# Weight blocks stored column by column in turn, and weight loads that take every other column

## The chip, the cores and the metric

The kernel runs on one core of one Trainium2 chip. The metric is the device time of one execution in microseconds (us). The kernel before took 3267.18 us, the median of three runs from 3265.66 to 3271.96 us. A core has a TensorE (PE, the matrix engine), a VectorE (DVE), a ScalarE (ACT), a GpSimd (POOL) and a SyncE (SP), which here only issues transfers. SBUF is the on-chip memory of 128 partitions that all of them read.

## The reference

The reference is a chain of transformer layers over one sequence of 256 tokens with a model width of 1024 in float32. There are two layers with half feed-forward blocks around a sparse attention and an RWKV mixer, a hybrid layer (state space and attention, then attention to a memory, with layer norms), and two layers over 272 tokens (16 meta tokens added) with a gated linear attention and a sliding-window attention. Most of the arithmetic is in feed-forward blocks of this kind, ten of them:

```python
def macaron_half_ffn(x, pre_g, post_g, w_gate, w_up, w_down):
    h = rmsnorm(x, pre_g)
    h = (jax.nn.silu(h @ w_gate) * (h @ w_up)) @ w_down
    return x + 0.5 * rmsnorm(h, post_g)
```

with `w_gate` and `w_up` of 1024 x 2816 and `w_down` of 2816 x 1024.

## The kernel before

**Tiling.** Activations lie transposed, features on the partitions and tokens along the free axis: `X[:, k, 0:T]` is block k of 128 features for T = 256 (or 272) tokens. A product is computed as output block (128 features x T tokens) = sum over k of (weight block 128 x 128) times (activation block 128 x T). The weight block is what TensorE loads (LDWEIGHTS, PEld in the profile), and the activation block is what it streams (MATMUL, PE).

**Three matmuls for one.** Weights and activations are split into a high part, rounded to the matrix engine's fast float32 format, and a low part, the rest. `mm3` (L187) issues high weight x high activation, high weight x low activation and low weight x high activation. Each issues its own weight load, and so the two in a row with the same high weight load it twice.

**Units.** Weights come from DRAM in units of 128 partitions x 1024 floats (512 KB), laid out by the host before the launch. `colunits` (L4296) makes a unit that holds the eight 128 x 128 blocks of one output block. `rowunits` (L4301) makes a unit of 128 rows of the weight with its 1024 columns, the eight blocks of eight output blocks. In both, block k is the 128 neighbouring floats k*128 to k*128+127 of each partition.

**The ring.** Class `Weights` (L200) holds eight raw slots and five slots for high parts; the low part overwrites the raw unit. SP issues the transfers in order (`load`, L240) and waits for `done`, which the last matmul of a unit raises. ACT rounds the raw unit (`hi`, L247), DVE subtracts for two of three units and POOL for the third (`low`, L256), each over the whole 1024 contiguous floats. A few units near the end of a product have their high part in spare slots instead.

**Who takes blocks.** `col` (L237) gives block k of a unit, high and low. It is used by `Ffn.firsts` (L981), `Ffn.unit` (L995), `Mixer.lin` (L1146), `Mixer.first` (L1157) and others. `Down.pe` (L927) slices its blocks itself. Some products use the weights as the streamed operand instead, 512 columns at a time: the RWKV projections (L1734), the values of the memory attention (L3153) and a few more. These read `views` of a unit and stream it.

**Addresses.** Buffers begin at chosen places within a row of 256 bytes: streamed activations at byte 64 (`PHASE`, L22), weights at byte 128 (`WPHASE`). A slot of 1024 floats is 4096 bytes, a block 512 bytes, and an activation block of 256 floats 1024 bytes, so that every block keeps its buffer's place in that row. With 272 tokens the blocks of most buffers are 320 floats apart, 1280 bytes, which keeps the place too.

**Order.** There is no planner. Each stage's methods `pe`, `act`, `dve`, `pool` give every engine its program in order, and semaphores tie them. In a feed-forward block TensorE computes gate and up blocks, 24 matmuls for a unit, then the down product.

Of the kernel before, what the change touches and what calls it, by code (L numbers as in the profile page):

```python
# [8 lines left out]
P = 128  # L9
# [190 lines left out]
class Weights:  # L200
# [34 lines left out]
        return self.his[w], self.lo_[:, r:r + UNIT]  # L235

    def col(self, w, k):  # L237
        return [x[:, k * P:(k + 1) * P] for x in self.views(w)]

    def load(self, sp, start, end=None):  # L240
        for w in range(start, len(self.units) if end is None else end):
# [32 lines left out]
    def need(self, pe, w):  # L274
        if w % 3 == 2:
            pe.wait_ge(self.cvp, w // 3 + 1)
        else:
            pe.wait_ge(self.cvl, w - w // 3 + 1)
# [5 lines left out]
class K:  # L284
# [31 lines left out]
    def hold(self, pe, bank, n):  # L316

        for _ in range(n):
            pe.mm(self.ps[bank][:, 0:P], self.ident, self.ident)
# [132 lines left out]
class Store:  # L452
# [5 lines left out]
    def pe(self, pe):  # L458
        pass
# [447 lines left out]
class Down:  # L907
# [22 lines left out]
    def pe(self, pe):  # L930
        K, T, nk = self.K, self.T, self.nk
        ends = nk > 8
        groups = [range(3)] * ends + [(k,) for k in range(3 * ends, nk - 3)] + [range(nk - 3, nk)]
        for ks in groups:
            for n in range(8):
                if self.free and ks[0] == 0:
                    pe.wait_ge(*self.free(n))
                for k in ks:
                    K.W.need(pe, self.u + k)
                    pe.wait_ge(*self.ready(k))  # L940
                    w = [x[:, n * P:(n + 1) * P] for x in K.W.views(self.u + k)]
                    t = pe.mm3(self.ps(n)[:, 0:T], w, [x[:, k, 0:T] for x in self.src], k == 0, k == nk - 1)
                    if n == 7:
                        t.then_inc(K.W.done, 1)
                    elif k == nk - 1:
                        t.then_inc(self.fin.h, 1)
# [2419 lines left out]
class Gla(Mixer):  # L3366
# [225 lines left out]
    def part(self, act, h):  # L3592
        act.wait_ge(*self.og(h))
        act.act(self.mix[0][:, 2 * h:2 * h + 2, 0:T3], self.os[:, h % 3], ACT.Copy).then_inc(self.oh.h, 1)
# [698 lines left out]
            store.pe(pe)  # L4293


def colunits(w):  # L4296
    k, n = w.shape
    return w.reshape(k // P, P, n // P, P).transpose(2, 1, 0, 3).reshape(n // P, P, k)


def rowunits(w):  # L4301
    k, n = w.shape
    return w.reshape(k // P, P, n)


def tiled(a):

    return a.reshape(len(a), D // P, P).transpose(2, 1, 0).reshape(P, -1)


def layout(v):
    d = {"x": tiled(v["x"][0]), "cst": constants(), "meta_tokens_3": tiled(v["meta_tokens_3"])}
    cols = np.zeros((P, NCOL + P), np.float32)
    cols[:, NCOL:] = np.concatenate([v["l0_cmp_w2_k"], v["l0_cmp_w2_v"]], 1)
    for name, (at, n) in COLS.items():
        a = np.repeat(v["d_skip_2"].reshape(-1), 64) if name == "d_skip_2c" else v[name]
        cols[:, at:at + n] = np.asarray(a).reshape(n, P).T
    d["cols"] = cols
    d["rows"] = np.concatenate([np.asarray(v[n]).reshape(1, 16) for n in ROWS], 1)
    for f in FFNS:  # L4320
        d[f + "_w_gate"] = colunits(v[f + "_w_gate"])
        d[f + "_w_up"] = colunits(v[f + "_w_up"])
        d[f + "_w_down"] = rowunits(v[f + "_w_down"])
    for f in ("ffn1", "ffn2"):
        w = v[f + "_w_in_2"][0]
        d[f + "_w_gate_2"] = colunits(w[:, :FF])
        d[f + "_w_up_2"] = colunits(w[:, FF:])
        d[f + "_w_out_2"] = rowunits(v[f + "_w_out_2"][0])
    for a in range(2):
        for b in range(2):  # L4330
            w = v["w_ffn_in_3"][a, b]
            d[f"g3_{a}{b}"] = colunits(w[:, :FF])
            d[f"u3_{a}{b}"] = colunits(w[:, FF:])
            d[f"d3_{a}{b}"] = rowunits(v["w_ffn_out_3"][a, b])
    w = v["l0_w_in"]
    c = np.cumsum([0, 512, 24, 128, 128, 128, 128, 128, 128, 512, 512, 512])
    part = lambda i: w[:, c[i]:c[i + 1]]
    d["nsa_in"] = colunits(np.concatenate([part(i) for i in (0, 2, 3, 4, 6, 8, 9, 10)], 1))
    d["nsa_v"] = np.concatenate([part(5), part(7)], 1).reshape(2, 4, P, 256).transpose(0, 2, 1, 3).reshape(2, P, UNIT)
    d["nsa_g"] = part(1).reshape(8, P, 24).transpose(1, 0, 2).reshape(P, 192)  # L4340
    for s in "kv":
        d["cmp_w1_" + s] = v["l0_cmp_w1_" + s].reshape(16, P, P).transpose(1, 0, 2).reshape(P, SLOT)
    d["nsa_out"] = rowunits(v["l0_w_out"])
    d["lora1"] = np.concatenate([v["l1_w_dec1"], v["l1_w_a1"], v["l1_w_g1"]], 1).reshape(8, P, 256).transpose(
        1, 0, 2).reshape(P, SLOT)
    d["lora2"] = np.concatenate([np.concatenate([v["l1_w_dec2"], v["l1_w_a2"]], 1),
                                 np.concatenate([v["l1_w0"], v["l1_a0"]])[None]], 0)
    d["l1_w_g2"] = v["l1_w_g2"]
    for n in ("l1_w_r", "l1_w_k", "l1_w_v", "l1_w_o"):
        d[n] = rowunits(v[n])  # L4350
    for n in ("l1_k_k", "l1_k_a", "l1_r_k", "l1_lnx_g", "l1_lnx_b"):
        d[n] = v[n].reshape(1, D)
    w = v["w_in_2"][0]
    c = np.cumsum([0, 1024, 1024, 1024, 2048, 16, 1024, 256, 1024, 64, 16])
    part = lambda i: w[:, c[i]:c[i + 1]]
    for i, n in ((0, "g_ssd"), (1, "g_att"), (2, "z_2"), (3, "xbc"), (5, "q_2"), (6, "ckv"), (7, "qidx")):
        d[n] = colunits(part(i))
    d["tokw"] = np.concatenate([part(4), part(9)], 1).reshape(8, P, 32).transpose(1, 0, 2).reshape(P, 256)
    d["kidx"] = part(8).reshape(8, P, 64).transpose(1, 0, 2).reshape(P, 512)
    d["w_uk"] = v["w_uk_2"][0].transpose(2, 0, 1).reshape(2, P, D)  # L4360
    d["w_uv"] = v["w_uv_2"][0].transpose(1, 0, 2).reshape(2, P, D)
    for n in ("w_proj_ssd_2", "w_proj_att_2", "w_out_2"):
        d[n] = rowunits(v[n][0])
    d["mem_2"] = tiled(v["mem_2"][0])
    d["mq"] = colunits(v["w_mq_2"][0])
    d["mk"] = colunits(v["w_mkv_2"][0][:, :D])
    d["mv"] = rowunits(v["w_mkv_2"][0][:, D:])
    d["w_mo"] = rowunits(v["w_mo_2"][0])
    w = v["gla_w_in_3"][0]
    d["gla_qk"] = colunits(w[:, :1024])  # L4370
    d["gla_v"] = colunits(w[:, 1024:2048])
    d["gla_r"] = colunits(w[:, 2048:3072])
    d["gla_lr"] = w[:, 3072:].reshape(8, P, 16).transpose(1, 0, 2).reshape(P, 128)
    d["gla_gate"] = v["gla_w_gate_3"][0]
    d["gla_out"] = rowunits(v["gla_w_out_3"][0])
    d["w_kv"] = colunits(v["w_kv_3"])
    d["swa_q"] = colunits(v["swa_w_q_3"][0])
    d["swa_out"] = rowunits(v["swa_w_out_3"][0])
    return {n: np.ascontiguousarray(a) for n, a in d.items()}


# [9 lines left out]
```

## Time and profile before

| | |
|---|---|
| Median of the runs | 3267.18 us |
| Span of the profiled execution | 3253.4 us |
| PE busy | 3111.1 us (96%), 27478 matmuls |
| PEld busy | 2988.1 us (92%), 27478 weight loads |
| DVE, ACT, POOL busy | 55%, 47%, 28% |
| DMA | 484.55 MB, mean 149 GB/s |
| Mean granted TensorE clock | 0.977 of full speed |

The profile gives no time of its own for the profiled execution beyond its span; the median lies 13.8 us above the span. The table gives shares of the span. Matmuls overlap each other in the records, and a PE that is busy for 96% says only that some matmul is nearly always in flight. The pace is to be read from the distance between the starts of matmuls, in the timeline, or from the number of matmuls that a view of windows counts in a stretch. A window counts each matmul that overlaps it, so the distance is the window's length plus one matmul's duration, divided by the count.

### The profile page before, as it was taken

The numbers are of one execution on the slowest core, as the hardware profiler recorded it, in microseconds if no ns is written. First come the engines' busy times: TensorE is split into PE (matmuls) and PEld (weight loads), VectorE is DVE, ScalarE is ACT, GpSimd is POOL, SyncE is SP. The second block draws the span as 40 slices with busy tenths as digits, with TensorE's granted clock in tenths as the row PEclk, the third lists the DMA queues.
The fourth block names the chain that finished last, engine by engine and source line by source line (L and its number), as shares of the span: only waits on it lengthen the run. The fifth ranks groups of instructions, "written<-read, shape, count | busy, mean of one in ns | idle before, by whom it ended". The sixth has DMA issues, their size and how long they took to land.

```text
span 3253.4 us, 64299 instructions
## 1 busy us (share of the span) xinstructions
PE 3111.1 (96%) x27478; PEld 2988.1 (92%) x27478; DVE 1803.0 (55%) x3040; ACT 1523.1 (47%) x2564; POOL 907.7 (28%) x481
## 2 busy tenths in 40 slices
PE   8999999999899999998999999999989999998999
PEld 8998899998688999998898889999979999997898
DVE  5456555647765645447567544454543546556554
ACT  5444454543422544437656444444333544544453
POOL 3321132331333232322221213222213332332232
PEclk9999999999999999999999999999989999998999
DMA  6542355564201555553343435535423454552354
GB/s 241 194 167 87 117 195 169 196 194 161 91 3 34 185 193 175 184 184 122 125 156 110 137 133 195 189 134 177 136 91 104 169 176 145 192 182 71 113 193 136
DMA packets 133388, 484.55 MB, mean 149 GB/s; under 512 B 14959, under 2 KB 17151, under 8 KB 132399
## 3 DMA queue, kind: packets, MB, share of 16 engines
q1 hardware_dynamic: 131120, 470.25, 43.1%
q0 software_dynamic: 1984, 10.19, 1.0%
q8 instruction: 217, 3.56, 0.4%
q14 instruction: 67, 0.55, 0.1%
HBM read 479.34 MB, written 1.05 MB: 148 GB/s over the span
## 4 chain that ended last, share of the span: by engine, by line
PE 82%; DVE 10%; ACT 5%; issue 2%; POOL 1%; DMA 0%; DVEq 0%; SPq 0%; ACTq 0%; POOLq 0%
PE ps L185 81%; DVE lo L162 2%; ACT hi L182 1%; ACT arena L182 1%; DVE tmp L170 1%; PE ps L193 1%; DVE sq L162 1%; DVE arena L170 1%; ACT L182 1%; DVE yT L170 1%; DVE arena L162 1%; POOL small L162 1%; POOL lo L162 0%; DVE small L179 0%; DVE xT L162 0%
## 5 line engine op out<-in xcount | busy, mean ns | idle before, releaser
L162 POOL TENSOR_TENSOR lo<-raw,hi 128x1024 fp32r<-128x1024 f32 x271 | 689.7, 2545 | 1683.3 <-ACT hi L182 1683.3
L182 ACT ACTIVATE hi<-raw 128x1024 fp32r<-128x1024 f32 x814 | 854.0, 1053 | 419.7 <-PE ps L185 312.2
L185 PE MATMUL ps<-hh,lo 128*128 128x256 f32 x3696 | 1019.5, 279 | 0.0
L162 DVE TENSOR_TENSOR lo<-raw,hi 128x1024 fp32r<-128x1024 f32 x543 | 703.7, 1299 | 513.6 <-ACT hi L182 493.4
L185 PE MATMUL ps<-hh,hi 128*128 128x256 f32 x3456 | 961.9, 281 | 24.3 <-ACT arena L182 8.8
L185 PE MATMUL ps<-hl,hi 128*128 128x256 f32 x3456 | 928.0, 279 | 1.2 <-DVE hl L162 1.2
L185 PEld LDWEIGHTS ps<-hh,lo 128*128 128x128 f32 x3696 | 702.6, 190 | 0.0
L185 PEld LDWEIGHTS ps<-hh,hi 128*128 128x128 f32 x3456 | 658.1, 190 | 32.8 <-ACT arena L182 12.2
L185 PEld LDWEIGHTS ps<-hl,hi 128*128 128x128 f32 x3456 | 641.6, 190 | 1.6 <-DVE hl L162 1.4
L185 PE MATMUL ps<-hfh,lo 128*128 128x256 f32 (+1 forms) x1760 | 489.5, 278 | 0.0
L185 PE MATMUL ps<-hfh,hi 128*128 128x256 f32 (+1 forms) x1520 | 422.7, 278 | 0.0
L185 PE MATMUL ps<-hfl,hi 128*128 128x256 f32 (+1 forms) x1520 | 422.7, 278 | 0.0
L185 PEld LDWEIGHTS ps<-hfh,lo 128*128 128x128 f32 x1760 | 330.6, 188 | 0.0
L185 PEld LDWEIGHTS ps<-hfh,hi 128*128 128x128 f32 x1520 | 285.5, 188 | 0.0
L185 PEld LDWEIGHTS ps<-hfl,hi 128*128 128x128 f32 x1520 | 285.5, 188 | 0.0
L162 DVE TENSOR_TENSOR tmp<-tmp,ps 128x256 f32<-128x256 f32 (+1 forms) x220 | 93.3, 424 | 309.9 <-PE ps L185 284.2
L185 PE MATMUL ps<-arena 64*64 64x64 f32 (+9 forms) x2992 | 227.4, 259 | 33.0 <-DVE arena L162 12.9
L185 PE MATMUL ps<-wh,lo 128*128 128x272 f32 x896 | 256.9, 289 | 0.0
L185 PE MATMUL ps<-wh,hi 128*128 128x272 f32 x848 | 246.6, 293 | 3.7 <-DVE arena L162 2.4
L185 PEld LDWEIGHTS ps<-arena 64*64 64x64 f32 (+4 forms) x2992 | 177.9, 153 | 76.8 <-issue 34.8
L185 PE MATMUL ps<-wl,hi 128*128 128x272 f32 x848 | 236.2, 289 | 0.0
L182 ACT ACTIVATE arena<-ps 128x256 f32<-128x256 f32 (+6 forms) x297 | 113.6, 403 | 248.8 <-PE ps L185 187.1
(385 smaller groups left out, 4716.6 us busy)
## 6 DMA issues: line engine op xcount, KB each, us to landing
raw<-in_l_ffn_w_gate SPq DMA_DIRECT2D x88, 512.0 KB, 3.3
raw<-in_l_ffn_w_up SPq DMA_DIRECT2D x88, 512.0 KB, 3.4
raw<-in_l_ffn_w_down SPq DMA_DIRECT2D x88, 512.0 KB, 3.6
raw<-in_g SPq DMA_DIRECT2D x88, 512.0 KB, 3.3
raw<-in_u SPq DMA_DIRECT2D x88, 512.0 KB, 3.3
raw<-in_d SPq DMA_DIRECT2D x88, 512.0 KB, 3.3
raw<-in_ffn_w_gate SPq DMA_DIRECT2D x44, 512.0 KB, 3.4
raw<-in_ffn_w_up SPq DMA_DIRECT2D x44, 512.0 KB, 3.5
```

The costliest lines, as they stand in the source:

```text
L162: return self.e.tensor_tensor(o, a, b, op)
L170: return self.e.scalar_tensor_tensor(o, a, s, b, op0, op1)
L182: return self.e.activation(o, a, f, **kw)
L185: return self.e.matmul(o, a, b, start=first, stop=final, skip_group_check=loose)
L193: return self.e.transpose(o, a, ident)
```

## The change

Two neighbouring 128-column blocks of a unit are interleaved: the first float is column 0 of the even block, the second column 0 of the odd block, the third column 1 of the even block, and so on. The host does it (`paired`), for all units whose blocks TensorE loads as weights. Units that are streamed (`rowunits` of the RWKV projections r, k, v, of `mv`, `w_uk`, `w_uv`, `nsa_v`) keep their layout. `col` gives the view that takes every other float of the pair, and `Down.pe` now uses `col`. The number and order of all instructions, transfers, waits and buffers is the same.

```diff
     def col(self, w, k):
-        return [x[:, k * P:(k + 1) * P] for x in self.views(w)]
+        c = k // 2 * 2 * P
+        return [x[:, c:c + 2 * P].rearrange("p (m j) -> p j m", j=2)[:, k % 2, :] for x in self.views(w)]
...
                     pe.wait_ge(*self.ready(k))
-                    w = [x[:, n * P:(n + 1) * P] for x in K.W.views(self.u + k)]
+                    w = K.W.col(self.u + k, n)
...
+def paired(u):
+
+
+    a, b, n = u.shape
+    return u.reshape(a, b, n // 256, 2, P).transpose(0, 1, 2, 4, 3).reshape(a, b, n)
+
+
 def colunits(w):
     k, n = w.shape
-    return w.reshape(k // P, P, n // P, P).transpose(2, 1, 0, 3).reshape(n // P, P, k)
+    return paired(w.reshape(k // P, P, n // P, P).transpose(2, 1, 0, 3).reshape(n // P, P, k))
...
+def downunits(w):
+    return paired(rowunits(w))
...
-        d[f + "_w_down"] = rowunits(v[f + "_w_down"])
+        d[f + "_w_down"] = downunits(v[f + "_w_down"])
...
-    for n in ("l1_w_r", "l1_w_k", "l1_w_v", "l1_w_o"):
+    for n in ("l1_w_r", "l1_w_k", "l1_w_v"):
         d[n] = rowunits(v[n])
+    d["l1_w_o"] = downunits(v["l1_w_o"])
```

The other products whose weights are loaded from `rowunits` change in the same way.

## Rows read from the trace of the kernel before

**Rows 1.** The page: busy time of the engines, then the chain that ended last.
```profile
PE 3111.1 (96%) x27478; PEld 2988.1 (92%) x27478; DVE 1803.0 (55%) x3040; ACT 1523.1 (47%) x2564; POOL 907.7 (28%) x481
...
PE 82%; DVE 10%; ACT 5%; issue 2%; POOL 1%; DMA 0%; DVEq 0%; SPq 0%; ACTq 0%; POOLq 0%
```

**Rows 2.** Windows: stretch, length, busy (count) of PE, PEld, DVE, ACT, POOL, PEclk, DMA.
```profile
600.00:730.00 130.00, 130.00 (x1149) 130.00 (x1148) 64.35 (x81) 61.96 (x82) 43.17 (x17) 1.00 0.60 193
...
2570.00:2650.00 80.00, 80.00 (x651) 80.00 (x650) 39.61 (x59) 37.41 (x54) 23.66 (x9) 1.00 0.54 178
...
3080.00:3240.00 160.00, 160.00 (x1415) 160.00 (x1414) 80.39 (x109) 75.55 (x106) 50.48 (x19) 1.00 0.52 174
```

**Rows 3.** Timeline of PE, 30 columns streamed after full loads: start us, us, engine, line, op.
```profile
244.27 0.28 PE L185 MATMUL ps<-hh,lo 128*128 128x256 f32 x1
244.39 3.65 PE L185 MATMUL ps<-arena,par 128*128 128x30 f32 x32
247.88 0.36 PE L185 MATMUL ps<-hh,hi 128*128 128x256 f32 x1
```

**Rows 4.** Timeline of PE: transposes, 128 columns streamed, eight merged.
```profile
317.69 1.04 PE L193 MATMUL ps<-cst,arena 128*128 128x128 f32 x8
```

**Rows 5.** Windows: first and last of the stretches with the longer distance, and others.
```profile
27.70:30.20 2.50, 2.50 (x24) 2.50 (x23) 0.62 (x2) 2.09 (x3) 0.00 (x0) 1.00 0.61 210
210.20:221.10 10.90, 10.90 (x95) 10.90 (x94) 4.86 (x15) 2.52 (x6) 0.00 (x0) 1.00 0.01 2
...
1488.00:1493.00 5.00, 5.00 (x45) 5.00 (x44) 4.93 (x6) 4.66 (x9) 2.29 (x1) 1.00 0.49 171
...
3060.80:3071.40 10.60, 10.60 (x92) 10.60 (x92) 9.64 (x25) 7.77 (x15) 0.00 (x0) 1.00 0.00 0
```

**Rows 6.** Window and timeline of PE at the lower granted clock.
```profile
1808.20:1811.10 2.90, 2.90 (x15) 2.90 (x15) 1.88 (x2) 0.00 (x0) 1.30 (x1) 0.50 0.01 3
...
1809.70 0.41 PE L185 MATMUL ps<-mTh,hi 128*128 128x256 f32 x1
1809.92 0.41 PE L185 MATMUL ps<-mTl,hi 128*128 128x256 f32 x1
1810.13 0.41 PE L185 MATMUL ps<-mTh,lo 128*128 128x256 f32 x1
1810.34 0.41 PE L185 MATMUL ps<-mTh,hi 128*128 128x256 f32 x1
```

**Rows 7.** Groups of PE by form: names, array, shape, count, busy us, mean ns.
```profile
L185 PE MATMUL ps<-hh,lo 128*128 128x256 f32 x3696 | 1019.5, 279 | 0.0
L185 PE MATMUL ps<-hh,hi 128*128 128x256 f32 x3456 | 961.9, 281 | 24.3 <-ACT arena L182 8.8 <-DVE hl L170 6.9 <-DVE lo L162 4.9
L185 PE MATMUL ps<-hl,hi 128*128 128x256 f32 x3456 | 928.0, 279 | 1.2 <-DVE hl L162 1.2
L185 PE MATMUL ps<-hfh,lo 128*128 128x256 f32 x1408 | 388.6, 276 | 0.0
...
L185 PE MATMUL ps<-wh,lo 128*128 128x272 f32 x896 | 256.9, 289 | 0.0
...
L185 PE MATMUL ps<-hfh,lo 128*128 128x272 f32 x352 | 100.8, 286 | 0.0
```

**Rows 8.** Timeline of PE, weights streamed 512 columns wide; first and last of ten starts.
```profile
770.89 0.39 PE L185 MATMUL ps<-hi,hh 128*128 128x512 f32 x1
...
772.95 0.39 PE L185 MATMUL ps<-hi,hh 128*128 128x512 f32 x1
```

**Rows 9.** Groups: what the engines do for each weight unit; page, part 5.
```profile
L162 POOL TENSOR_TENSOR lo<-raw,hi 128x1024 fp32r<-128x1024 f32 x271 | 689.7, 2545 | 1683.3 <-ACT hi L182 1683.3
L182 ACT ACTIVATE hi<-raw 128x1024 fp32r<-128x1024 f32 x814 | 854.0, 1053 | 419.7 <-PE ps L185 312.2
...
L162 DVE TENSOR_TENSOR lo<-raw,hi 128x1024 fp32r<-128x1024 f32 x543 | 703.7, 1299 | 513.6 <-ACT hi L182 493.4
```

More of the change, by code:

```diff
@@ L4327, in layout @@
         d[f + "_w_up_2"] = colunits(w[:, FF:])
-        d[f + "_w_out_2"] = rowunits(v[f + "_w_out_2"][0])
+        d[f + "_w_out_2"] = downunits(v[f + "_w_out_2"][0])
     for a in range(2):
@@ L4333, in layout @@
             d[f"u3_{a}{b}"] = colunits(w[:, FF:])
-            d[f"d3_{a}{b}"] = rowunits(v["w_ffn_out_3"][a, b])
+            d[f"d3_{a}{b}"] = downunits(v["w_ffn_out_3"][a, b])
     w = v["l0_w_in"]
@@ L4342, in layout @@
         d["cmp_w1_" + s] = v["l0_cmp_w1_" + s].reshape(16, P, P).transpose(1, 0, 2).reshape(P, SLOT)
-    d["nsa_out"] = rowunits(v["l0_w_out"])
+    d["nsa_out"] = downunits(v["l0_w_out"])
     d["lora1"] = np.concatenate([v["l1_w_dec1"], v["l1_w_a1"], v["l1_w_g1"]], 1).reshape(8, P, 256).transpose(
@@ L4362, in layout @@
     for n in ("w_proj_ssd_2", "w_proj_att_2", "w_out_2"):
-        d[n] = rowunits(v[n][0])
+        d[n] = downunits(v[n][0])
     d["mem_2"] = tiled(v["mem_2"][0])
@@ L4367, in layout @@
     d["mv"] = rowunits(v["w_mkv_2"][0][:, D:])
-    d["w_mo"] = rowunits(v["w_mo_2"][0])
+    d["w_mo"] = downunits(v["w_mo_2"][0])
     w = v["gla_w_in_3"][0]
@@ L4374, in layout @@
     d["gla_gate"] = v["gla_w_gate_3"][0]
-    d["gla_out"] = rowunits(v["gla_w_out_3"][0])
+    d["gla_out"] = downunits(v["gla_w_out_3"][0])
     d["w_kv"] = colunits(v["w_kv_3"])
     d["swa_q"] = colunits(v["swa_w_q_3"][0])
-    d["swa_out"] = rowunits(v["swa_w_out_3"][0])
+    d["swa_out"] = downunits(v["swa_w_out_3"][0])
     return {n: np.ascontiguousarray(a) for n, a in d.items()}
```

## The prediction

> **What bounds the kernel now.** I read the page's busy times and the chain that ended last first [rows 1]: the chain is PE for 82%, and waits of PE for other engines are small. DVE, ACT and POOL are busy for 55, 47 and 28%, and DMA has no share of the chain. So the time is the number of matmuls times the distance between their starts, plus some 18% of chain outside PE that the change doesn't touch.
>
> The distance comes next, from the windows [rows 2]. In 600 to 730 us, (130 + 0.28) / 1149 = 113.4 ns; in 3080 to 3240 us, 160.28 / 1415 = 113.3 ns. Both stretches stream 256 columns. In 2570 to 2650 us, with 272 columns, it is 80.28 / 651 = 123.3 ns. At the lower clock the starts are 0.64 / 3 = 213 ns apart for 256 columns [rows 6], that is one column per 1/1.2 ns and nothing beside it; at the clock of 2.4 GHz 256 columns alone would take 106.7 ns and 272 columns 113.3 ns. Hence 6.6 ns of each 113.3, and 10 ns of each 123.3, are not streaming.
>
> What else takes time is the weight load. When only 30 columns are streamed after a full 128 x 128 load, 32 matmuls take from 244.39 to 247.88 us [rows 3]: the last of them is followed closely, so the row's own length is the better measure, (3.65 - 0.19) / 31 = 111.6 ns, with 0.19 as the duration of a matmul of 30 columns: 0.28 less 226 columns at 0.417 ns. The load by itself thus sets a beat of 111.6 ns, and the 256-column matmuls stand 1.7 ns above it. Transposes with the same load have (1.04 - 0.28) / 7 = 109 ns [rows 4].
>
> Then there is something that is neither. In some stretches the same instructions on the same buffers run at a longer distance [rows 5]: 11.18 / 95 = 117.7 ns, 5.28 / 45 = 117.3 ns, 10.88 / 92 = 118.3 ns. At 210 us DMA is at 1% and POOL and ACT nearly idle, at 1488 us DVE and ACT are nearly full, and the distance is the same; and the clock is full in all. So it isn't another engine. What is left is TensorE against itself: its two streams out of SBUF, the load and the streamed operand, in different relation to each other. Counted over the timeline about 1,100 distances of 256-column matmuls lie there, from the stretch at 27.70 to the one at 3060.80 [rows 5], and about 15,000 lie at 113. The 512-column matmuls show it too: nine distances in 2.06 us, 229 ns, where the columns alone are 213.3 [rows 8].
>
> **The two paces.** At the full clock the streamed operand passes 4 bytes per 0.417 ns and partition, the load 4 bytes per about 0.83 ns. In one matmul the streamed operand goes through four rows of 256 bytes, the load through two. If SBUF is divided so that the place within the row decides, the faster stream overtakes the slower twice per matmul whatever the two begin with. At the lower clock both go at 0.83 ns per float, and there the rows show no loss at all [rows 6], though the load has slack there, so this is a hint and no proof. After the change the load passes 8 bytes per column, four rows per load: the paces are equal at the full clock and nobody overtakes.
>
> **Part by part.**
> *Instructions, waits, transfers:* same number, same bytes per transfer (4096 contiguous bytes per partition), same order. ACT's and DVE's and POOL's passes go over the whole unit and don't see the order of columns [rows 9]. I cost all this at nothing. The cover that a faster TensorE needs is there: a unit is 24 matmuls, 2.72 us now and 2.68 us after, for 1.05 us of ACT, 2/3 x 1.3 = 0.87 us of DVE and 1/3 x 2.55 = 0.85 us of POOL, and DMA has 0.52 to 0.60 of its share [rows 2]. Only short stretches like 1488 to 1493 us, where DVE has 4.93 of 5 us [rows 5], have no cover; if the distance falls there, DVE is late next, and at 45 matmuls times 6 ns that is 0.3 us, which I leave out.
>
> *256 columns:* the groups with a weight unit as load [rows 7] are 3696 + 3456 + 3456 + 1408 and the two partners of the last with 1216 each, 14,448, and smaller groups with 1,900 more. Of these 16,400 some 15,000 lie at 113.3. If the overtaking ends they fall to the load's beat of 111.6, 1.7 ns each: 15,000 x 1.7 = 25 us. The 1,100 at 117.7 fall by 6.1 ns: 7 us. The rest is at the lower clock, or begins a stretch, and stays.
>
> *272 columns:* 896 and 352 for the low weights and about twice as many for the high ones [rows 7], some 3,900 at the full clock. Here the columns are longer than the load. I take the columns plus the same 5 ns that the load's beat has over its 106.7 (128 columns at 1.2 GHz): 118.3 instead of 123.3, so 3,900 x 5 = 20 us.
>
> *Sum:* 25 + 7 + 20 = 52 us. Against the profiled execution: 3253.4 - 52 = 3201 us of span; with the 13.8 us between span and median, 3215 us.
>
> *Bounds of the one unknown cost,* a load that takes every other float. The trace before has no such load. From the good side the transposes' 109 ns bound it, 2.4 ns over the columns: 15,000 x 4.3 + 1,100 x 8.7 + 3,900 x 7.6 = 65 + 10 + 30 = 104 us, 3163 us. From the bad side the nearest row is the longer distance, if all matmuls fall into it: 15,000 x 4.4 = 66 us, and 3,900 x 4.4 = 17 us, 3350 us. The farthest row is the load at half pace, 213 ns for each [rows 6]: 19,000 x 100 ns, over 5,000 us. I take the load as no slower in itself, because the streamed operand already reads 8 bytes in the time of one load column, and so does the load after the change.
>
> The Trainium skill ("SBUF — State Buffer", Specifications) says that SBUF has lines of 16 bytes and that two hits in a line are needed for full bandwidth. Every other float of a line of four is exactly two hits, so by the letter the change is free, but it stands on the edge. No row here shows a load with fewer hits than four.
>
> **Rivals.**
> *A, nothing changes.* The 113.3 is a fixed beat of loading and starting, and the relation of the streams doesn't matter. For it: the beat is the same over 130 and 160 us, whatever block of the unit is loaded [rows 2]. Against it: two distances for the same instructions [rows 5]. Time 3267 us. The same page ("Who interferes with whom") gives TensorE two independent read ports and says that it never waits on anyone; by this rule the change would give 3267 us, and the two distances speak against it only as far as TensorE against itself.
>
> *B, the streams lock into each other.* With equal pace a meeting of the two doesn't pass: where the load starts at the same place of the row as the streamed operand, it stays there for the whole load. The buffers' places are 64 bytes apart, which is 16 columns, and a load starts about as the matmul before it starts, so they should miss each other, but a lag of some 7 ns (64 bytes at 4 bytes per 0.417 ns) between the two makes them meet. It decides if a meeting costs more than one shift that then parts them. Price: the longer distance for all, +83 us, 3350 us.
>
> *C, the load pays for the floats it skips.* Suppose it fetches neighbours in groups, say of four floats. Before, 128 columns are 32 fetches and each float is used; after, they are 64, and two of four are the other block's. If each further fetch costs a column's time of 0.83 ns [rows 6], that is 32 x 0.83 = 27 ns on the load's beat, 111.6 + 27 = 138 ns; against 113.3 and 123.3 this is 16,000 x 25 + 3,900 x 15 = 460 us, 3725 us. Speaking for it, the 512-column matmuls lose 16 ns where the streamed operand passes four times a load's bytes [rows 8]; against it, nothing is lost at the lower clock [rows 6]. It decides as soon as a second fetch can't be made while two columns are loaded. The same page, under Specifications, says that "each cross to a new line pays a penalty"; taken alone that is this rival, and taken with its two hits it is the forecast.
>
> **How the numbers follow.** Forecast (a gain between 20 and 104 us) 0.52; A 0.18; B 0.20; C and what is worse 0.10. A measurement of this kernel tells 0.2%, 6.5 us, from no change. Faster 0.52, same 0.18, slower 0.30. The likeliest is 3215 us, its own range 3163 to 3247 us. The range that holds 8 of 10 reaches from 3163 to 3352 us: it takes in A and most of B, and leaves out C.
>
> **What would show it.** Right: in a dense stretch such as 3080 to 3240 us the windows count 1438 or more matmuls in 160 us (111.6 ns) instead of 1415, about 678 in 80 us with 272 columns, and no stretches at 117.7; the 512-column matmuls stay at 229 ns, since their weights keep the layout. A is shown by the same counts as before. B shows as a distance of 117 ns or more over long stretches, C as one of 130 ns or more and a duration of the weight load above its neighbours'. The forecast is wrong if the dense distance doesn't fall below 113, or if it falls and the time is given back in waits of TensorE for DVE's or ACT's parts of a unit.

## The result and the profile after

The changed kernel takes 3360.83 us (median of four runs, 3356.75 to 3368.33), against 3266.42 us of the kernel before beside it. The ratio is 1.0292 with an interval of 1.0255 to 1.0329: 2.9% slower, 94 us. The forecast was 3215 us. A ratio here and below compares a kernel with runs of the kernel before taken beside it, and it can differ a little from the quotient of two medians. A time "by the ratio" is the ratio times 3266.42 us.

The head of the page after, to be held against [rows 1]: engine busy times, then the chain that ended last.

```profile
span 3366.5 us, 64299 instructions
...
PE 3234.9 (96%) x27478; PEld 3109.4 (92%) x27478; DVE 1792.4 (53%) x3040; ACT 1521.0 (45%) x2564; POOL 908.6 (27%) x481
...
PE 85%; DVE 8%; ACT 4%; issue 2%; POOL 1%; DMA 0%; SPq 0%; DVEq 0%; ACTq 0%; POOLq 0%
```

The number of instructions is the same, and DVE, ACT and POOL are busy for the same time within 0.6%. PE's busy time grew by 124 us, the span by 113. So TensorE got slower at the same work, and its share of the chain rose. The windows of the kernel after (stretch, length, busy and count of PE, PEld, DVE, ACT, POOL, clock, DMA share, GB/s) over stretches of the same kind as in [rows 2]:

```profile
620.00:750.00 130.00, 130.00 (x1086) 130.00 (x1085) 59.84 (x77) 59.48 (x78) 39.08 (x16) 1.00 0.57 183
2650.00:2730.00 80.00, 80.00 (x634) 80.00 (x633) 38.18 (x58) 36.47 (x54) 23.74 (x9) 1.00 0.52 172
3180.00:3340.00 160.00, 160.00 (x1335) 159.97 (x1334) 77.69 (x104) 75.48 (x103) 50.55 (x20) 1.00 0.56 182
```

130.28 / 1086 = 120.0 ns and 160.28 / 1335 = 120.1 ns where it was 113.4 and 113.3; 80.28 / 634 = 126.6 ns with 272 columns where it was 123.3. The clock is full in all. Counted over the whole timeline, the distances of 256-column matmuls in a row are 16,233 before with a mean of 113.66 ns and 16,271 after with 119.99 ns: 1845.1 us became 1952.3 us, 107 more. Those of 272 columns went from 485.4 to 497.2 us, 12 more. Everything else fell by 6 us. 107 + 12 - 6 = 113 us is the difference of the spans, so waits and transfers together add nothing to it. The medians are only 94 us apart: the traced execution before lies 13.8 us below its median, and the traced one after is the slowest of its four.

### The profile page after: what moved, and what is told of

Read it like the earlier page. It is cut to its first block, busy times and chain, and to the rows that moved or that the text cites. A ratio compares the mean times of both kernels' runs of the same rounds, so it can differ in the third digit from the quotient of the medians.

```text
span 3366.5 us, 64299 instructions
## 1 busy us (share of the span) xinstructions
PE 3234.9 (96%) x27478; PEld 3109.4 (92%) x27478; DVE 1792.4 (53%) x3040; ACT 1521.0 (45%) x2564; POOL 908.6 (27%) x481
## 4 chain that ended last, share of the span: by engine, by line
PE 85%; DVE 8%; ACT 4%; issue 2%; POOL 1%; DMA 0%; SPq 0%; DVEq 0%; ACTq 0%; POOLq 0%
PE ps L185 84%; DVE lo L162 1%; ACT arena L182 1%; ACT hi L182 1%; DVE tmp L170 1%; PE ps L193 1%; DVE sq L162 1%; ACT L182 1%; DVE arena L162 1%; DVE arena L170 1%; POOL small L162 1%; DVE yT L170 0%; POOL lo L162 0%; DVE hT_hi L162 0%; DVE xT L162 0%
## 5 line engine op out<-in xcount | busy, mean ns | idle before, releaser
L185 PE MATMUL ps<-hh,lo 128*128 128x256 f32 x3696 | 1039.3, 284 | 0.0
L185 PE MATMUL ps<-hh,hi 128*128 128x256 f32 x3456 | 977.6, 285 | 23.1 <-ACT arena L182 8.3
L185 PE MATMUL ps<-hl,hi 128*128 128x256 f32 x3456 | 944.4, 283 | 0.6 <-DVE hl L162 0.6
L185 PEld LDWEIGHTS ps<-hh,lo 128*128 128x128 f32 x3696 | 721.8, 195 | 0.0
L185 PEld LDWEIGHTS ps<-hh,hi 128*128 128x128 f32 x3456 | 677.5, 196 | 31.4 <-ACT arena L182 11.5
L185 PEld LDWEIGHTS ps<-hl,hi 128*128 128x128 f32 x3456 | 660.4, 196 | 0.9 <-DVE hl L162 0.8
L185 PE MATMUL ps<-hfh,lo 128*128 128x256 f32 (+1 forms) x1760 | 499.5, 284 | 0.0
L185 PEld LDWEIGHTS ps<-hfh,lo 128*128 128x128 f32 x1760 | 340.6, 194 | 0.0
L185 PEld LDWEIGHTS ps<-hfh,hi 128*128 128x128 f32 x1520 | 295.2, 194 | 0.0
L182 ACT ACTIVATE hfh<-tmp 128x256 fp32r<-128x256 f32 (+1 forms) x220 | 92.4, 420 | 301.4 <-DVE tmp L162 300.2
```

The costliest lines, as they stand in the source:

```text
L182: return self.e.activation(o, a, f, **kw)
L185: return self.e.matmul(o, a, b, start=first, stop=final, skip_group_check=loose)
```

## The experiments

The texts of expectation name theories by letters. L and L' say that TensorE's two streams, the load and the streamed operand, meet and hold each other back. C and C' say that the load itself pays for the floats it skips. R is C' with a price, 1.82 ns for each group of four neighbouring floats that is touched. F adds to R that 256 streamed columns lose a quiet relation of the two streams. A "place" is the byte at which the streamed operand begins, counted from the load's within 256 bytes.

**The first small kernel: places and columns.** Loads at the step of one or two floats, the streamed operand at sixteen places. Its core, shortened, repeated 48 times a stretch, each time with the next bank:

```python
pe.matmul(banks[:, i % 8, 0:n], w(k), m[:, k * pitch:k * pitch + n], start=True, stop=True)
```

> A kernel of its own that computes none of the reference: 48 matmuls in a row per stretch, each with its own 128 x 128 load, first with the load's columns contiguous, then with every other float of a pair of blocks. Streamed are 256, 272, 128 and 512 columns; the streamed operand begins at each multiple of 16 bytes within a row of 256 bytes (of 64 bytes for 128 and 512 columns), the loads at byte 0. At the end 16 columns are streamed after loads of either kind. Theory L (the two streams of TensorE meet and hold each other back): with every other float the distance depends on the begin, near 111.7 ns at most begins and clearly above 118 ns at some, while contiguous loads stay at 113 to 118 at all begins; with 16 columns streamed both kinds of load take 111.7 ns. Theory C (the load pays for the floats it skips): every other float costs the same number of ns more at every begin, and with 16 columns streamed its distance is also above 111.7, by 6 ns or more.

Windows of that kernel (PE, PEld, ACT, POOL): its end, 16 columns after loads at a step of two; then 128 columns streamed after contiguous loads and after loads at a step of two; then 256 columns at place 192 after contiguous loads.

```profile
543.00:552.00 9.00, 9.00 (x44) 9.00 (x44) 0.00 (x0) 0.00 (x0) 0.50 0.00 0
404.00:408.50 4.50, 4.50 (x43) 4.50 (x42) 0.00 (x0) 0.00 (x0) 1.00 0.00 0
409.50:414.30 4.80, 4.80 (x43) 4.80 (x43) 0.00 (x0) 0.00 (x0) 1.00 0.00 0
165.00:170.00 5.00, 5.00 (x45) 5.00 (x44) 0.00 (x0) 0.00 (x0) 1.00 0.00 0
```

The windows of the small kernels are short, and a count in them tells a distance only to 1 part in 45; distances given to a tenth of a ns are means over the starts in the timeline. With 128 columns the distance between starts was 111.6, 111.6, 111.8 and 111.7 ns for contiguous loads at the four places, and 117.8, 118.3, 118.3 and 117.7 ns for loads at a step of two. That is 6 to 7 ns a load at every place: theory L is in trouble. With 256 columns the step of two gave 117.8 to 121.7 ns over the sixteen places, but contiguous loads spread too, from 114.1 to 120.0 ns, with 117.8 ns at place 192, where the kernel before has 113.3. With 272 columns contiguous loads gave 123.4 to 126.6 ns by place and loads at a step of two 124.5 to 128.4. The last stretch, which should have told most, was lost to the clock: 16 columns after contiguous loads stand 111.7 ns apart at the full clock, but it fell to half before the loads at a step of two began, and there both kinds stand 213 ns apart.

**Down's blocks contiguous again.**

```diff
-                    w = K.W.col(self.u + k, n)
+                    w = [x[:, n * P:(n + 1) * P] for x in K.W.views(self.u + k)]
...
-    return paired(rowunits(w))
+    return rowunits(w)
```

> The changed kernel, but the products that run through Down.pe keep contiguous blocks as before; gate, up and the mixers' projections load every other float. Some 5,900 of the 16,200 matmuls with 256 columns and 1,300 of the 3,900 with 272 go back. If the loss belongs to each load with every other float (either theory), they go back to 113.3 and 123.3 ns and the time is 3361 - 5900 x 6.6 ns - 1300 x 3.3 ns = 3318 us. If the loss were in only one kind of product, or in the engines beside it, it would be 3361 or 3267 us.

Windows of a down product in this kernel and in the changed one:

```profile
145.00:195.00 50.00, 50.00 (x443) 50.00 (x443) 21.16 (x15) 21.64 (x23) 17.16 (x7) 1.00 0.59 200
...
145.00:195.00 50.00, 50.00 (x419) 50.00 (x418) 20.70 (x13) 20.78 (x20) 15.93 (x7) 1.00 0.58 190
```

Measured: 3328.1 us, ratio 1.0169 (1.0134 to 1.0204), 3321 us by the ratio, with 3318 expected. The down products of all ten feed-forward blocks are back, at 113.3 ns with 256 columns and 123.3 with 272: 50.28 / 443 = 113.5 ns against 50.28 / 419 = 120.0 in the windows. In all 5,022 distances of 256 columns are back, where 5,900 were expected; the longer ones have a mean of 119.9 ns. The loss goes with the products whose loads are stepped.

**Steps of 1, 2, 3, 4 and 8 floats, then whole units.**

```python
return w[:, at:at + st * P].rearrange("p (m j) -> p j m", j=st)[:, k % st, :]
```

> A kernel of its own that computes none of the reference. First 16 and then 128 columns are streamed after loads whose 128 columns lie at steps of 1 (beginning at byte 0, 4 and 8), 2, 3, 4 and 8 floats. Then whole units of 24 matmuls as in the kernel (high, high, low weight of each block, 256 columns streamed into one bank), with loads at steps of 1, 2 and 4 and the streamed operand beginning 0, 64, 128 and 192 bytes after the load's place; the last is the kernel's own. In the first small kernel loads at a step of 2 were 6.3 ns dearer than contiguous ones with 128 columns streamed, at every begin. Theory C' (the load itself pays, 6.3 ns a load, whatever is streamed): with 16 columns the step of 2 gives 118 ns, the same at every begin; a step of 4 costs more than a step of 2, and steps of 4 and 8 cost the same if it is a matter of lines of four floats. Theory L' (the cost is the meeting of the two streams): with 16 columns, where hardly anything is streamed, the step of 2 gives 111.7 ns as the step of 1 does.

The timeline of PE in this kernel, 24 matmuls with 128 columns merged to a row each: steps 1 (beginning at byte 8), 2, 3, 4 and 8.

```profile
140.26 2.79 PE L72 MATMUL ps<-mbuf,wbuf 128*128 128x128 f32 x24
...
150.13 2.94 PE L72 MATMUL ps<-mbuf,wbuf 128*128 128x128 f32 x24
...
160.14 4.31 PE L72 MATMUL ps<-mbuf,wbuf 128*128 128x128 f32 x24
...
171.53 5.75 PE L72 MATMUL ps<-mbuf,wbuf 128*128 128x128 f32 x24
...
185.52 5.90 PE L72 MATMUL ps<-mbuf,wbuf 128*128 128x128 f32 x24
```

The mean distances of the starts are 111.6, 117.8, 175.5, 233.6 and 240 ns (the last at a mean clock of 0.92, the one before at 0.98; units at step 4 at the full clock gave 233.3). This is the curve of theory C': 128 columns touch 32 groups of four floats at step 1, 64 at step 2, 96 at step 3 and 128 at step 4 and beyond. 175.5 / 96 = 1.83 ns, 233.3 / 128 = 1.82 ns, 117.8 / 64 = 1.84 ns a group; step 8 touches no more groups than step 4 and costs little more. At step 1 the price of 32 groups would be 58 ns, far below the 111.7 measured, so something else is the limit there. When the clock falls to half within the row at step 8, the distance stays at 240 ns: this price doesn't follow TensorE's clock.

With whole units and 256 columns, the streamed operand 0, 64, 128 and 192 bytes after the load's place, contiguous loads gave 120.0, 117.8, 118.6 and 113.3 ns, loads at a step of two 120.0, 120.0, 121.1 and 120.1 ns. Here is the second half of the story. The 113.3 ns of the kernel before is not the beat of contiguous loads in general; of these four places only 192, the kernel's, has it. And place alone doesn't settle it, since the first small kernel had 117.8 ns at 192. With 16 columns the clock fell during the stretch at a step of two, but the nineteen distances before it fell have a mean of 117.8 ns, against 111.7 at step 1, so L' already fails here; the third small kernel repeats it at the full clock throughout.

**Streamed activations moved in the row, before and after the change.** The same one-line edit in both kernels; byte 192 of the row is 64 bytes after the load's, place 64:

```diff
-PHASE, WPHASE = 64, 128
+PHASE, WPHASE = 192, 128
```

> The kernel before with streamed activations placed at byte 192 of the 256-byte row instead of 64; loads stay at 128. Theory L: the distance depends on the place, so it moves away from 113.3 ns, towards 118 ns, and the time towards 3340 us. Theory C: contiguous loads don't care much, 3267 us within 15 us.

Measured: 3322.1 us against 3276.14 beside it, ratio 1.0153 (1.0126 to 1.018). 15,529 of its 16,263 distances of 256 columns are 116 ns or more, nearly all 117.8. Theory C's "don't care much" was wrong: a place alone costs the kernel before half of what the change cost.

> The changed kernel with streamed activations placed at byte 192 instead of 64. Theory L (with equal pace the place decides all): the distance moves by several ns, to 112 or to 125, and the time by 60 us or more. Theory C (each load pays): 120 ns and 3361 us stay within 15 us.

Measured: 3374.29 us, ratio 1.0304 (1.0272 to 1.0336), 3366 us by the ratio; mean distance 120.5 ns. With loads at a step of two this move of place changed it by half a nanosecond, as C said.

**The third small kernel: the load alone, fewer columns, all places.**

> A kernel of its own that computes none of the reference, at the full clock throughout. (a) 16 columns streamed after loads at steps of 1, 2, 2 and 4 floats. (b) Units of 24 matmuls as in the kernel, place 192 bytes after the load's, with 192, 224, 240, 248 and 256 columns streamed, loads at steps of 1 and 2. (c) Units with 256 columns and loads at steps of 1 and 2, and with 272 columns and step 1, the streamed operand beginning at each multiple of 16 bytes after the load's place. Theory R (each port of TensorE gets a group of four neighbouring floats every 1.82 ns at best, so that 64 groups take 117 ns and 128 take 233): (a) 111.7, 117.8, 117.8 and 233 ns; (b) step 2 stays at 117.8 ns down to 192 columns, because the load is the limit, while step 1 falls to 111.7; (c) step 2 between 117.8 and 122 ns at all sixteen places, step 1 below 117.8 only at a few places, of which 192 is one. Theory L' (only the meeting of the streams costs): (a) 111.7 for step 2, (b) step 2 falls towards 111.7 with fewer columns.

Timeline of PE there, 12 matmuls with 16 columns merged: step 1, 2, 2 and 4, all at the full clock.

```profile
34.96 1.40 PE L73 MATMUL ps<-mbuf,wbuf 128*128 128x16 f32 x12
...
43.36 1.47 PE L73 MATMUL ps<-mbuf,wbuf 128*128 128x16 f32 x12
...
51.58 1.47 PE L73 MATMUL ps<-mbuf,wbuf 128*128 128x16 f32 x12
...
59.80 2.86 PE L73 MATMUL ps<-mbuf,wbuf 128*128 128x16 f32 x12
```

(1.47 - 1.40) / 11 = 6 ns more per load with hardly anything streamed beside it. By the starts it is 111.67, 117.78, 117.78 and 233.6 ns. This is the load's own cost, and L' is out. (The fourth row, by a step of 4, is a check of the group price: 128 groups at 1.82 ns.) Windows of the same kernel: 192 columns at steps 1 and 2; 256 columns at step 1 and places 0, 64 and 192; 256 columns at step 2 and places 0, 80 and 192.

```profile
70.80:75.60 4.80, 4.80 (x45) 4.80 (x44) 0.00 (x0) 0.00 (x0) 1.00 0.00 0
77.00:82.20 5.20, 5.20 (x47) 5.20 (x45) 0.00 (x0) 0.00 (x0) 1.00 0.00 0
...
135.50:140.80 5.30, 5.30 (x46) 5.30 (x46) 0.00 (x0) 0.00 (x0) 1.00 0.00 0
161.90:167.10 5.20, 5.20 (x46) 5.20 (x45) 0.00 (x0) 0.00 (x0) 1.00 0.01 3
214.50:219.60 5.10, 5.10 (x48) 5.10 (x47) 0.00 (x0) 0.00 (x0) 1.00 0.00 0
240.70:246.00 5.30, 5.30 (x46) 5.30 (x46) 0.00 (x0) 0.00 (x0) 1.00 0.00 0
273.70:279.30 5.60, 5.60 (x50) 5.60 (x49) 0.00 (x0) 0.00 (x0) 1.00 0.00 0
320.80:326.10 5.30, 5.30 (x46) 5.30 (x45) 0.00 (x0) 0.00 (x0) 1.00 0.00 0
```

The distances of starts, in ns:

| columns streamed (place 192) | 192 | 224 | 240 | 248 | 256 |
|---|---|---|---|---|---|
| step 1 | 111.7 | 111.8 | 112.0 | 113.3 | 113.3 |
| step 2 | 118.3 | 118.7 | 117.8 | 117.8 | 120.1 |

| place, 256 columns | 0 | 16 | 32 | 48 | 64 | 80 | 96 | 112 |
|---|---|---|---|---|---|---|---|---|
| step 1 | 119.8 | 116.6 | 116.7 | 118.5 | 117.8 | 118.4 | 119.8 | 114.3 |
| step 2 | 120.0 | 118.4 | 121.0 | 120.0 | 120.0 | 117.8 | 120.0 | 120.0 |

| place, 256 columns | 128 | 144 | 160 | 176 | 192 | 208 | 224 | 240 |
|---|---|---|---|---|---|---|---|---|
| step 1 | 118.7 | 118.8 | 117.3 | 119.3 | 113.3 | 119.3 | 118.2 | 117.2 |
| step 2 | 120.0 | 120.0 | 120.6 | 119.0 | 120.1 | 120.0 | 120.0 | 119.9 |

Two things are to be read. At step 2 no place goes below 117.78 ns, the load's own beat; they lie between 117.8 and 121.0. At step 1 the mean over the places is some 118 ns, and 192 is the best of the sixteen, 112 the next. At 112 the distance is long only at first and is 113.35 ns in the second half of the stretch. So the kernel before stood in a quiet spot that two places in sixteen have. (Theory R's (c) had this right, with 16, 32, 112, 160 and 240 as the other places below 117.7.)

But even at place 192 contiguous loads have two beats. Between its rows of 16 columns this kernel has stretches of 60 identical matmuls, 256 columns after contiguous loads, all at place 192 and the full clock:

```profile
36.21 7.31 PE L68 MATMUL ps<-mbuf,wbuf 128*128 128x256 f32 x60
...
44.69 7.06 PE L68 MATMUL ps<-mbuf,wbuf 128*128 128x256 f32 x60
...
52.91 7.05 PE L68 MATMUL ps<-mbuf,wbuf 128*128 128x256 f32 x60
```

The first has 117.8 ns from its second distance to its end. The other two settle at 113.3 ns within five and keep it. These are the two distances of [rows 5], with no other engine at work.

**The interleaved layout with contiguous loads.**

```diff
-        c = k // 2 * 2 * P
-        return [x[:, c:c + 2 * P].rearrange("p (m j) -> p j m", j=2)[:, k % 2, :] for x in self.views(w)]
+        return [x[:, k * P:(k + 1) * P] for x in self.views(w)]
```

> The changed kernel with its interleaved units in DRAM and in the buffers, but each load takes 128 neighbouring floats again, so that the products mix columns of two blocks (the output is not the reference's). Theory R (the load's reads cost): 113.3 and 123.3 ns, 3267 us within 10 us, as before the change. If the layout in DRAM, the transfers or the passes of ACT, DVE and POOL had a part in the loss, it stays above 3290 us.

Measured: 3275.9 us against 3278.14 beside it, ratio 0.9997 (0.9975 to 1.002). A window of 256 columns in the kernel before, the same in this kernel, and one of this kernel with 272 columns, as long as that of [rows 2]:

```profile
380.00:550.00 170.00, 168.11 (x1480) 167.72 (x1480) 89.56 (x121) 84.53 (x115) 58.78 (x23) 1.00 0.59 196
...
380.00:550.00 170.00, 167.76 (x1478) 167.37 (x1476) 89.95 (x119) 85.05 (x119) 57.34 (x23) 1.00 0.57 192
...
2620.00:2700.00 80.00, 80.00 (x651) 80.00 (x650) 33.76 (x37) 34.25 (x41) 23.40 (x10) 1.00 0.53 180
```

The last has the 651 matmuls of before. The loss is gone with nothing but the read pattern of the loads. The layout in DRAM, the transfers and the other engines' passes have no part in it.

This trace also shows how long a beat lasts. The same window of feed-forward matmuls before and in this kernel:

```profile
1085.00:1240.00 155.00, 155.00 (x1370) 155.00 (x1370) 81.49 (x104) 76.56 (x103) 51.92 (x20) 1.00 0.59 195
...
1085.00:1240.00 155.00, 155.00 (x1318) 155.00 (x1318) 75.03 (x97) 72.73 (x97) 49.58 (x20) 1.00 0.57 187
```

155.28 / 1370 = 113.3 ns and 155.28 / 1318 = 117.8 ns, with the same places and contiguous loads in both. In this kernel the longer beat holds for 1,438 distances in a row. Of the 44 unbroken stretches of 25 and more such matmuls in the trace before, 34 run at 113.3 ns after their first few, nine at 117.8, and only one changes in between. The beat is settled where a stretch begins.

**Only the low weights at a step of two.**

```diff
-        return [x[:, c:c + 2 * P].rearrange("p (m j) -> p j m", j=2)[:, k % 2, :] for x in self.views(w)]
+        hi, lo = self.views(w)
+        return [hi[:, k * P:(k + 1) * P], lo[:, c:c + 2 * P].rearrange("p (m j) -> p j m", j=2)[:, k % 2, :]]
```

> As e4_whole_load, but the low weights are loaded at a step of two floats and the high ones, two of three loads, contiguously (again the output is not the reference's). Theory R, cost per load: of three distances one is 118 to 120 ns and two are 113.3, so a third of the loss, 3267 + 94 / 3 = 3298 us. If the streams lock, all three distances move, to 117.8 ns or more, and the time is 3330 to 3361 us.

Measured: 3360.69 us against 3278.14 beside it, ratio 1.0249 (1.0226 to 1.0272), 3348 us by the ratio: 85% of the loss with a third of the stepped loads. The window at 380 us, to be held against the 1478 matmuls of the kernel above:

```profile
380.00:550.00 170.00, 168.60 (x1405) 168.22 (x1404) 86.49 (x128) 82.12 (x116) 52.49 (x21) 1.00 0.53 180
```

Theory R fell here. The mean distance is 119.88 ns, and all three kinds moved: some 118 ns after low x high, 122 after high x high, 121 after high x low.

**Which of the three loads is stepped, by columns streamed.**

> A kernel of its own that computes none of the reference: units of 24 matmuls at the kernel's own places (streamed operand 192 bytes after the load's), with 192, 240 and 256 columns streamed, where none, the first high, the second high, the low, the last two or all three of a block's three loads go at a step of two floats. Theory F (a stepped load has a floor of its own of 117.8 ns, and beside it 256 columns lose the quiet relation that gives 113.3): with 192 columns the mean of three distances is 111.7, 113.7, 113.7, 113.7, 115.7 and 117.8, each stepped load costing its own 6 ns; with 256 columns one stepped load already lifts the mean from 113.3 to between 118 and 120, as in e5_low_step. Theory R (each stepped load pays its own and nothing else): with 256 columns one stepped load gives 113.3 + 2 = 115.5.

Windows of this kernel: 192 columns with no load, the low one and all three stepped, then 256 columns with the same three.

```profile
30.00:39.00 9.00, 9.00 (x83) 9.00 (x82) 0.00 (x0) 0.00 (x0) 1.00 0.01 2
...
66.00:75.00 9.00, 9.00 (x82) 9.00 (x80) 0.00 (x0) 0.00 (x0) 1.00 0.01 2
...
90.00:99.00 9.00, 9.00 (x78) 9.00 (x78) 0.00 (x0) 0.00 (x0) 1.00 0.00 0
173.00:183.00 10.00, 10.00 (x90) 10.00 (x90) 0.00 (x0) 0.00 (x0) 1.00 0.01 2
...
210.00:220.00 10.00, 10.00 (x85) 10.00 (x85) 0.00 (x0) 0.00 (x0) 1.00 0.00 0
...
235.00:245.00 10.00, 10.00 (x86) 10.00 (x85) 0.00 (x0) 0.00 (x0) 1.00 0.01 2
```

| mean distance, ns | none | first high | second high | low | last two | all |
|---|---|---|---|---|---|---|
| 192 columns | 111.7 | 114.4 | 113.9 | 113.9 | 116.7 | 118.3 |
| 240 columns | 113.3 | 114.4 | 114.4 | 114.4 | 116.7 | 117.8 |
| 256 columns | 113.3 | 120.0 | 120.0 | 120.0 | 118.9 | 120.0 |

With 192 columns one stepped load adds 2.2 to 2.7 ns to the mean of three, and all three add 6.6, near the 2 and 6 ns of theory F. With 256 columns the first stepped load takes everything: 113.3 becomes 120.0 ns, whichever of the three it is, and further ones add nothing.

**The changed kernel at the best place for stepped loads.** Byte 208 of the row, place 80:

```diff
-PHASE, WPHASE = 64, 128
+PHASE, WPHASE = 192, 128
...
-        return p3(self.alias(name, at, k * T)[:, :], k)
+        return p3(self.alias(name, at, k * T + 4)[:, 4:], k)
```

(and the same four floats in `over` for the hidden activations).

> The changed kernel with the feed-forward blocks' and most projections' streamed activations placed at byte 208 of the 256-byte row, 80 bytes after the load's. In the small kernel a step of two gave 117.78 ns there, its floor, instead of 120.1. Theory F: about 13,000 distances fall from 120 to 117.8 ns, 29 us, and those of 272 columns from 126.6 to 125, 6 us: 3361 - 35 = 3326 us, and no place brings it below 3320. If place doesn't matter for stepped loads: 3361 us.

Measured: 3332.74 us, ratio 1.0201 (1.0151 to 1.0251). Mean distances 117.96 and 125.12 ns, as the small kernel had them; by the ratio the time is 3332 us (3316 to 3348), with 3326 expected. A window of it, against the 120.0 ns of the change: 110.28 / 937 = 117.7 ns.

```profile
3150.00:3260.00 110.00, 110.00 (x937) 110.00 (x936) 56.91 (x80) 52.77 (x75) 35.84 (x14) 1.00 0.56 183
```

This is the changed layout at the best of the sixteen places and still 2% slower than before, because 117.8 is the load's floor. The 28 us that it wins over the change are the place's part. No version that was run beats the kernel before, and by the table of places moving the streamed operand alone wouldn't: 113.3 ns is the lowest of the sixteen.

## Why the prediction was wrong

The change was forecast to save 52 us and cost 94; 3361 us lies 9 us above the range, whose upper end took in most of rival B. The frame held: the time is matmuls times distance, layout, transfers and other engines cost nothing (e4_whole_load), the counts of affected matmuls were right, and the 512-column matmuls, whose weights kept their layout, didn't change. The rate fell where I had written "I take the load as no slower in itself, because the streamed operand already reads 8 bytes in the time of one load column". Three steps failed.

*That step.* It put the load's own cost at nothing. A load at a step of two takes 117.8 ns instead of 111.7 even with only 16 columns streamed beside it (m3_fine). The argument by the streamed operand was void, for the streamed operand shows a like limit: 512 columns take 229 ns [rows 8], which is 128 groups of four floats at 1.79 ns, and 272 columns take 123.3 ns [rows 2], 68 groups at 1.81 ns. I had the 16 ns of loss at 512 columns and read it as overtaking. By rows I could have seen that the load would have to fetch 64 groups, and that at 1.79 to 1.81 ns these take 115 to 116 ns, more than 111.6. That 256 columns are held by their groups too is not shown: 248 and 256 columns both have 113.3 ns (m3_fine).

*"If the overtaking ends they fall to the load's beat of 111.6."* That the 1.7 ns between 111.6 and 113.3 are a price of overtaking is shown by nothing, and they didn't fall away. The two streams do disturb each other, and by more than I thought: with contiguous loads 256 columns have 113.3 to 120 ns by place (m2_strides, m3_fine, e2_before_p192). The two distances of [rows 5] were rightly read as TensorE against itself, but 113.3 is the quiet side of it, not the disturbed one. Equal paces brought no quiet: stepped loads have 117.8 to 121.0 ns over the places (m3_fine). With 272 columns, which I had falling to 118.3 ns, 126.7 came; the load's floor of 117.8 lies below the 123.3 from before and can't be what raised it by 3.3 ns, so that loss lies between the two streams. Contiguous loads alone have 123.4 to 126.6 ns there by place (m1_phases).

*"At the lower clock both go at 0.83 ns per float".* They don't. At the lower clock 16 columns after a full load stand 213 ns apart (the first window of m1_phases, with stepped loads; five distances of contiguous loads just before it, at the same clock, are 213 to 215), so the load goes at 1.67 ns per column there, half the pace of the stream as at the full clock. The load has no slack there either. What stood in the prediction as a hint for equal paces was no case of equal paces.

Of the rivals, B had the time, 3350 against 3361 us, but only partly the mechanism. It priced the other distance, 117.7 ns, where 120.0 came, and no place showed a meeting that stays at a price of its own: stepped loads move by 3.2 ns over the sixteen places (m3_fine) and by 0.5 between places 64 and 192 (e3_after_p192). What does lock are contiguous loads, at 113.3 or 117.8 ns for a whole stretch (e4_whole_load). C had the mechanism of the larger part, fetches of groups of four floats, and the wrong price: at 1.82 ns 64 groups take 117 ns, so that doubling the fetches cost 6 ns and not 27.

How much is which? With 256 columns and all loads stepped, the floor of 117.8 is 4.5 of the 6.7 ns from 113.3 to 120.0; e6_after_p208 shows it, with the place chosen so that only the floor is left: 117.96 ns. The other 2 ns are the streams' disturbance at the kernel's own place. But the two causes don't add: with one load stepped in three, where floors would give 115, the distance is 120 (m4_mixed, e5_low_step).

What stays open is by what rule the streams disturb each other: why 192 is quiet, why one stepped load in three ends it with 256 columns and not with 240, and what at the start of a stretch decides between 113.3 and 117.8 ns [rows 5]. Even 240 columns with contiguous loads gave 112.0 ns in m3_fine and 113.3 in m4_mixed. The number of distances of 116 ns and more differs between kernels with the same pattern of reads: 1,151 before, 3,508 in e4_whole_load, 2,357 more at 4.4 ns, or 10 us, and the traced span is 8.4 us longer. The medians, of 10 and 13 runs, don't differ. So the beats may fall differently from one execution to the next, but each kernel was traced once and this isn't shown.

## What to carry to other kernels

The load of a read pattern is best judged by how many groups of four neighbouring float32 it touches: about 1.8 ns each here, so that 64 groups just exceed what 128 contiguous columns take anyway. Before giving such a pattern to a whole kernel, measure it alone in a stretch of 48 matmuls, with few columns streamed and then with the kernel's own places and column count. Start such a stretch several times, since the same matmuls can settle on two beats. A beat that is better than its neighbours' may be a lucky relation of two streams; ask what would end it before touching either.

## What the runs showed of the hardware

The load: 111.7, 117.8, 175.5, 233.6 and about 240 ns for 128 columns at steps of 1, 2, 3, 4 and 8 floats. At the lower clock a step of two cost nothing: 213 ns for either kind (m1_phases). The streamed operand pays alike: 256 columns at a step of two took 230 ns (m2_strides), as much as 512 contiguous ones. The Trainium skill ("SBUF — State Buffer", Specifications) gives lines of 16 bytes, which is the group seen here, and says that two hits in a line are enough for full bandwidth. The measurement differs: two hits cost the load 6.1 ns of 111.7, and a full-clock stream isn't at full bandwidth with four (512 columns in 229 instead of 213.3 ns).

The place of the streamed operand against the load's within 256 bytes moved 256-column matmuls between 113.3 and 120 ns, and at one and the same place there were two beats, 113.3 and 117.8. By the same page of the Trainium skill ("Who interferes with whom") TensorE's two read ports are independent. The measurement differs: moving only the streamed operand cost the kernel before 1.5% (e2_before_p192), and the small kernels show it with no other engine at work.
